# Hybrid decoder block on one core: the second feed-forward matmul as seven block products, with its weight sums on VectorE and GpSimd

## What is computed

```python
h = rms_norm(x, g_ffn_norm[l])
x = x + jnp.square(jax.nn.relu(h @ w_ff1[l])) @ w_ff2[l]
```

## Time and profile before

| | us |
|---|---|
| median of 3 runs | 633.36 (633.29 to 633.74) |
| the profiled execution, its own time | 633.49 |
| its span, first to last instruction | 631.8 |
| PE busy | 617.6 (98%) |
| DVE busy | 325.5 (52%) |
| ACT busy | 264.6 (42%) |
| POOL busy | 11.0 (2%) |

### The profile page before, as it was taken

The page is one execution under the profiler, slowest core; times in us unless marked ns, Lnnn a source line. Parts: engine busy times, 40 slices in busy tenths (PEclk is TensorE's granted clock), DMA queues, the critical chain, the costliest instruction groups (busy, mean ns, idle before and its releaser), DMA issues.

```text
span 631.8 us, 8695 instructions
## 1 busy us (share of the span) xinstructions
PE 617.6 (98%) x3130; PEld 515.5 (82%) x3130; DVE 325.5 (52%) x577; ACT 264.6 (42%) x503; POOL 11.0 (2%) x31
## 2 busy tenths in 40 slices
PE   7999999999999999999999999999999999999997
PEld 5888677788898888988888888888888888888885
DVE  5699981686688686564333333334433333333323
ACT  7656552737466656462222222223333333222220
POOL 1400000000000000000000000000000000000000
PEclk9999999999999999999999999999999999999999
DMA  8512447342121020004223322332222323322003
GB/s 341 181 42 66 134 137 262 102 167 67 34 68 67 0 68 1 1 1 139 95 99 100 100 100 100 100 98 94 87 89 100 100 100 100 100 100 97 36 0 134
DMA packets 17228, 60.08 MB, mean 95 GB/s; under 512 B 2144, under 2 KB 2432, under 8 KB 17200
## 3 DMA queue, kind: packets, MB, share of 16 engines
q1 hardware_dynamic: 16416, 57.88, 27.0%
q0 software_dynamic: 640, 1.82, 0.9%
q10 hardware_dynamic: 144, 0.01, 0.0%
HBM read 57.60 MB, written 2.10 MB: 94 GB/s over the span
## 4 chain that ended last, share of the span: by engine, by line
PE 91%; DVE 4%; ACT 2%; issue 1%; POOL 0%; DVEq 0%; ACTq 0%; POOLq 0%
PE ps L317 26%; PE ps L319 25%; PE ps L318 25%; PE ps L1687 4%; PE ps L1675 2%; PE ps L1636 1%; PE ps L1422 1%; PE ps L1545 1%; PE ps L1637 1%; DVE ht_lo L955 1%; PE ps L1508 1%; PE ps L1617 1%; DVE w_lo_sb L933 1%; ACT ht_hi L564 1%; PE ps L1597 1%
## 5 line engine op out<-in xcount | busy, mean ns | idle before, releaser
L317 PE MATMUL ps<-ht_hi,w_hi_sb 128*128 128x512 f32 (+1 forms) x280 | 107.7, 385 | 0.0
L319 PE MATMUL ps<-ht_hi,w_lo_sb 128*128 128x512 f32 (+1 forms) x280 | 107.3, 383 | 0.0
L318 PE MATMUL ps<-ht_lo,w_hi_sb 128*128 128x512 f32 (+1 forms) x280 | 107.3, 383 | 0.0
L317 PE MATMUL ps<-w_hi_sb,a_hi 128*128 128x512 f32 x256 | 99.6, 389 | 0.0
L318 PE MATMUL ps<-w_lo_sb,a_hi 128*128 128x512 f32 x256 | 99.6, 389 | 0.0
L319 PE MATMUL ps<-w_hi_sb,a_lo 128*128 128x512 f32 x256 | 99.6, 389 | 0.0
L317 PE MATMUL ps<-w_hi_sb,ht_hi 128*128 128x512 f32 x192 | 82.1, 427 | 3.0 <-DVE ht_lo L955 1.6
L1293 DVE TENSOR_TENSOR w_lo_sb<-raw,w_hi_sb 128x1024 fp32r<-128x1024 f32 x64 | 78.3, 1225 | 10.2 <-ACT w_hi_sb L809 5.0
L319 PE MATMUL ps<-w_hi_sb,ht_lo 128*128 128x512 f32 x192 | 75.3, 392 | 0.0
L318 PE MATMUL ps<-w_lo_sb,ht_hi 128*128 128x512 f32 x192 | 75.1, 391 | 0.0
L1358 DVE TENSOR_TENSOR act_sb<-act_sb (+1 forms) x32 | 22.2, 692 | 102.8 <-ACT act_sb L891 102.8
(11 more groups left out here) (189 smaller groups left out, 791.0 us busy)
## 6 DMA issues: line engine op xcount, KB each, us to landing
raw<-in_w_ff SPq DMA_DIRECT2D x64, 512.0 KB, 3.4
raw<-in_w SPq DMA_DIRECT2D x24, 512.0 KB, 4.6
xs<-in_x SPq DMA_DIRECT2D x8, 512.0 KB, 6.7
raw<-in_cmp_w SPq DMA_DIRECT2D x8, 512.0 KB, 4.7
out_y<-xs SPq DMA_DIRECT2D x3, 512.0 KB, 2.7
raw<-in_w_c SPq DMA_DIRECT2D x4, 304.0 KB, 2.8
spw_sb<-in_sp_w POOLq DMA_DIRECT2D x1, 512.0 KB, 3.6
grow_ffn<-in_g_ffn POOLq DMA_DIRECT2D x1, 512.0 KB, 3.8
```

The lines of the kernel that those rows point to most:

```text
L317: pe.matmul(out, l_hi, r_hi, start=start, stop=False)
L318: pe.matmul(out, l_hi, r_lo, start=False, stop=False)
L319: return pe.matmul(out, l_lo, r_hi, start=False, stop=stop)
```

## The change

The second matmul is cut into quadrants: rows of the activations in two halves (256 each), the hidden dimension in two halves (16 units of 128 each), output columns in two halves (512 each). One level of Strassen's scheme (Winograd's form) gives the four output quadrants by seven products of quadrant size and sums of quadrants before and after. Unit J of the hidden dimension now stands for rows J and J + 16 of `w_ff2`.

- **Products.** Group 1, sixteen steps: P1, P5, P6, P4 (4 products x 2 row tiles x 3 passes = 24 matmuls of 128x512 a step). Group 2, sixteen steps: P3, P2, P7 (18 matmuls a step). In all 672 matmuls where there were 768.
- **Activation sums.** Kept for all units in `aq` (six pieces of 256 a unit). DVE makes three sums of 256 for each unit while the first matmul runs (`sums`), and one more after each group-1 step (`fourth_sum`).
- **Weight sums, group 1.** For each step three differences of 128x512, in place in `raw`: DVE makes the first (`t1_form`) for the next step, POOL the second and third (each waits for the one before it). Group 2 has one, on DVE (`t3_form`), and loads `w_ff2` once more (768 KB a step).
- **Partial results.** Between the groups P1, P6, P5 and P4 are taken out of PSUM and combined in `part`; four `base` instructions add them into `xs` during group 2.
- The tiles are laid out anew in SBUF; the work before the second matmul is otherwise the same.

The diff, cut to what the change does in time (line numbers of the changed file are those that the extracts below it use):

```diff
+A11, S1, A22, S2, A12, A21 = range(6)
+S4, S3 = S2, A21
+FIRST = slice(A11, S2 + 1)
+SECOND = slice(S4, S3 + 1)
+PRODUCTS = {"P1": (A11, 0, 0, 0), "P5": (S1, 0, 1, 2), "P6": (S2, 1, 0, 4), "P4": (A22, 1, 1, 6),
+            "P3": (S4, 0, 0, 2), "P2": (A12, 0, 1, 0), "P7": (S3, 1, 0, 4)}
+G1, G1_LAST = ["P1", "P5", "P6", "P4"], ["P1", "P6", "P5", "P4"]
+G2, G2_FIRST = ["P3", "P2", "P7"], ["P2", "P3", "P7"]
...
         @block.gpsimd
...
+            with pool.Fori(0, HF // 2) as i:
+                for j in range(2):
+                    a, b = 2 * j, 2 * j + 1
+                    n = i * 4 + 2 * j
+                    pool.wait_ge(raw_in[b], i * 16 + (IN + 16))
+                    pool.wait_ge(t1_made, i * 2 + (j + 1))
+                    pool.tensor_tensor(raw[:, b, b1], raw[:, b, b1], raw[:, a, b2], ALU.subtract).then_inc(t_made, 1)
+                    pool.wait_ge(t_made, n + 1)
+                    pool.tensor_tensor(raw[:, b, b2], raw[:, b, b1], raw[:, b, b2], ALU.subtract).then_inc(t_made, 1)
...
         @block.scalar
...
+            def first_group(j, J):
+                form_hi(2 * j, J * 2 + (U0 - 3), made_1=J + 1)
+                form_hi(2 * j + 1, J * 2 + (U0 - 2), J * 2 + 2)
+                a_high(j, J, FIRST, J * 2 + (U0 - 2), J * 3 + 3)
...
         @block.vector
...
+            def t1_form(j, loaded):
+                a, b = slice(0, 512), slice(512, 1024)
+                dve.wait_ge(raw_in[2 * j], loaded)
+                dve.tensor_tensor(raw[:, 2 * j, b], raw[:, 2 * j, b], raw[:, 2 * j, a], ALU.subtract).then_inc(t1_made, 1)
...
+            def first_group(j, J, nxt):
+                form_lo(2 * j, J * 2 + (H0 + 1))
+                form_lo(2 * j + 1, J * 2 + (H0 + 2))
+                nxt()
+                a_low(j, J, FIRST, J + 1)
+                fourth_sum(J, J + 1)
...
+            def second_group(j, i):
+                J = i * 2 + (HF + j)
+                form_lo(2 * j, J * 2 + (H0 + 1))
+                form_lo(2 * j + 1, J * 2 + (H0 + 2), 512)
+                t3_form(1 - j, i * 16 + (T3_IN + 16 * j))
+                a_low(j, i * 2 + j, SECOND, J + 1)
...
+            with dve.Fori(1, HF // 2 - 1) as i:
+                first_group(0, i * 2, lambda: t1_form(1, i * 16 + (IN1 + 16)))
+                first_group(1, i * 2 + 1, lambda: t1_form(0, i * 16 + (IN1 + 32)))
+            first_group(0, HF - 2, lambda: t1_form(1, IN1 + 16 * (HF // 2)))
+            first_group(1, HF - 1, lambda: t3_form(0, T3_IN))
+            second_group(0, 0)
+            dve.wait_ge(p1_kept, 1)
+            dve.wait_ge(p_whole, 2)
+            dve.tensor_tensor(part[:, :, 1, :], ps[:, 4:6, :], part[:, :, 0, :], ALU.add).then_inc(kept, 1)
...
+            dve.tensor_tensor(part[:, :, 2, :], ps[:, 2:4, :], part[:, :, 1, :], ALU.add).then_inc(kept, 1)
+            second_group(1, 0)
+            dve.wait_ge(w_used, U0 + 2 * HF)
+            dve.tensor_tensor(part[:, :, 1, :], part[:, :, 1, :], ps[:, 6:8, :], ALU.subtract).then_inc(kept, 1)
...
+            for t in range(4):
+                second_group(t % 2, 1 + t // 2)
+                base(t)
...
         @block.tensor
...
+            def step(j, J, products, first=False, last=False):
+                units = [PRODUCTS[p][1] for p in products]
+                pe.wait_ge(al_done, J + 1)
+                for n, p in enumerate(products):
+                    unit = units[n]
+                    if unit not in units[:n]:
+                        pe.wait_ge(w_lo, J * 2 + (NS + NF + 1 + unit))
...
+                    for i in range(2):
+                        mm = piece(j, p, i, first, last)
+                    if unit not in units[n + 1:]:
+                        mm.then_inc(w_used, 1)
```

More of the change, by code:

```diff
@@ new lines, in _ @@
+                if j % 2:
+                    a_high(j // 2, j // 2, FIRST, NW + NF - (2, 0)[j // 2], 3 * (j // 2) + 3)
+            with act.Fori(1, HF // 2) as i:
+                for j in range(2):
+                    first_group(j, i * 2 + j)
+            second_group(0, 0)
+            act.wait_ge(p_whole, 1)
+            act.activation(part[:, :, 0, :], ps[:, 0:2, :], ACT.Copy).then_inc(p1_kept, 1)
+            second_group(1, 0)
+            with act.Fori(1, HF // 2 - 1) as i:
+                for j in range(2):
+                    second_group(j, i)
@@ L919, in _ @@
+            for j in range(2):
+                second_group(j, HF // 2 - 1, skew=j == 1)
         @block.vector
@@ new lines, in _ @@
+                if j == 1:
+                    sums(NF // FR - 1, 1)
+                if j % 2:
+                    a_low(j // 2, j // 2, FIRST, j // 2 + 1)
+            sums(NF // FR - 1, FR - 1)
+            for J in range(2):
+                fourth_sum(J, J + 1)
+            t1_form(0, IN1 + 32)
+            with dve.Fori(1, HF // 2 - 1) as i:
+                first_group(0, i * 2, lambda: t1_form(1, i * 16 + (IN1 + 16)))
+                first_group(1, i * 2 + 1, lambda: t1_form(0, i * 16 + (IN1 + 32)))
@@ L1399, in _ @@
+            dve.wait_ge(based, 4)
+            for n, (p, i) in enumerate(ENDED):
+                dve.wait_ge(m_done, n + 1)
+                for c in LAST_COLS if n == len(ENDED) - 1 else [slice(0, 512)]:
+                    result(p, i, c)
         @block.tensor
@@ new lines, in _ @@
+            step(0, 0, G1, first=True)
+            step(1, 1, G1)
+            with pe.Fori(1, HF // 2 - 1) as i:
+                for j in range(2):
+                    step(j, i * 2 + j, G1)
+            step(0, HF - 2, G1)
+            step(1, HF - 1, G1_LAST, last=True)
+            step(0, HF, G2_FIRST, first=True)
+            step(1, HF + 1, G2)
+            with pe.Fori(1, HF // 2 - 1) as i:
+                for j in range(2):
+                    step(j, i * 2 + (HF + j), G2)
+            seen = set()
@@ L1812, in _ @@
+            for n, (p, i, e) in enumerate(LAST_TWO):
+                unit, J = PRODUCTS[p][1], 2 * HF - 2 + e
+                if e not in seen:
+                    pe.wait_ge(al_done, J + 1)
+                    seen.add(e)
+                if (e, unit) not in seen:
+                    pe.wait_ge(w_lo, 2 * J + NS + NF + 1 + (unit if e == 0 else 1 - unit))
+                    seen.add((e, unit))
+                mm = piece(e, p, i, False, e == 1)
+                if e:
                     mm.then_inc(m_done, 1)
@@ L1844, in layouts @@
     wo = i["w_out"][0]
+    w2 = i["w_ff2"][0].reshape(NF, P, D)
     return {
```

264 lines of the change are left out of this document (168 added, 96 removed).

## The result

The changed kernel takes 637.25 us (median of 6 runs, 636.27 to 638.02) against 633.37 (633.28 to 634.64) for the kernel before: a ratio of 1.0057, interval 1.0042 to 1.0071. It removes 96 matmuls worth 21.8 us and is 0.6% **slower**. The profiled execution took 637.98 us by its own time.

What follows compares the result with a forecast made beforehand. PE alone was taken to bound the second matmul, and the feeding group 1 after the change. 633.5 - 21.8 (matmuls) + 25.5 (group 1, with step 2's 3.7) + 2.8 (group 2) = 640.0 us; range 624 to 655.

Steps and rivals of the forecast that it cites:

- The mechanism: Second matmul, group 1: POOL and DVE exclude each other, so feeding becomes the bound; PE idles 1.2 to 2.2 us a step.
- Matmuls removed, -21.8: Second matmul: 96 of 768 matmuls removed at 0.2267 us each, all on the path, -21.8 us.
- the ring: Group-1 cycle of waits: POOL's pair, ACT's hi copy, DVE's second lo, `t1_form`, POOL's next pair; 7.1 us against PE's 5.44.
- POOL's duration h: Group 1: time of one POOL difference of 512, bounded by 0.95 and 1.56 us, taken as 1.1.
- Whether POOL and DVE block each other: Group 1: two-SBUF-input DVE instructions and POOL's take turns by whole instructions, read from one encounter in the trace before.
- Rival 1: Group 1: POOL and DVE do not hinder each other, ring 5.44 us, total 617.3 us; chance 0.16.
- POOL first: Group-1 ring: POOL's second difference goes ahead of DVE's first lo; next cycle at 6.6 us, total 633.1.
- DVE first: Group-1 ring: DVE's first lo goes ahead of POOL's second difference; next cycle at 7.65 us, total 647.0.
- Step 2 late, +3.7: Start of group 1: step 2's feeding is ready at 467.6, PE has ended steps 0 and 1 at 463.9; +3.7 us.
- Group 2, +2.8: First group-2 steps: seven extra 1024-element DVE instructions on `part` and `base` make steps 4.6 us; +2.8, between 1 and 6.
- Hidden, priced at nothing: First-matmul sums, POOL's pairs for steps 0 and 1, ReLU in two pieces, second `w_ff2` load: all hidden, 0 us.
- Tail, +-0.3: After the last matmul: a 256-column `result` and its 2.6 us DMA, the same two last as before; +-0.3 us.

Runs made afterwards that it cites:

- the run with 32 columns: The changed kernel with POOL's two differences on 32 columns in place of 512, waits kept: 619.71 us, ratio 0.977 to the kernel before.
- the run with aligned tiles: The changed kernel with 64 bytes left free ahead of the two weight tiles, so they start on multiples of 128: 632.39 us, ratio 0.9967.
- no GpSimd in the same order: The changed kernel with POOL's two differences moved to DVE, right behind the first one, order otherwise kept: 629.06 us, ratio 0.9913.
- earlier first difference: The changed kernel with DVE's difference for the next step put between the two weight lo parts, except at step 15: 635.21 us, ratio 1.0015.

## Where the prediction was right, where it was off, and what was luck

The mechanism was right, with its place and its engine, and 640.0 was 2.8 us too high, with the truth inside the range. That it came out slower, as forecast, was luck: what the mechanism and group 2 cost as measured is under the 21.8 us that the removed matmuls give, and with its weight tiles on multiples of 128 the same kernel is slightly faster than before. The sign and most of the closeness come from a cost that the forecast had priced at nothing.

- **Matmuls removed, -21.8:** as priced. The count of instructions (3034 against 3130) stands; so does the 5.44 us of PE's own work in a step, but for the tiles (5.60 in the odd steps, hidden by the ring).
- **POOL's duration h, taken 1.1 between 0.95 and 1.56:** 1.30 alone (443.76), and 1.13 to 1.16 counted from the moment that DVE lets go, which is what the ring's sum needed. The estimate worked out from the Trainium skill (GPSIMD Engine Reference, Elementwise: side-by-side cycle accounting), 1.12, agrees with the latter.
- **Whether POOL and DVE block each other:** yes, and by whole instructions, as the one encounter had said. The rule in the Trainium skill (SBUF — State Buffer, Who interferes with whom) holds in every meeting seen here. Rival 1 (617.3) falls with it, and the run with 32 columns is near what it would have given.
- **The ring, taken 7.1 a step:** this is **the term that was mis-sized**. The forecast had worked out 6.6 for POOL first and 7.65 for DVE first and took the middle (7.1; its sum has 5.44 + 1.68 = 7.12), since the rows before don't decide the order. It is 6.66: POOL's second is issued 0.08 us after its first ends (506.87 against 506.79), not 0.15 to 0.24 as the earlier trace rows gave, and so 0.13 ahead of DVE's lo. In every meeting read here the one that was issued first got the turn. The middle was worth 13 x 0.46 = 6.0 us too much. A middle of two discrete orders is a time that neither gives; by the forecast's own "POOL first" the sum was 633.1.
- **Step 2 late, +3.7:** 3.6. What the forecast did not have: behind this hole PE runs at its lower level for a while (granted clock 0.87 in the window of steps 2 and 3, whose 48 matmuls take 12.57 us from first to last start instead of 47 x 0.2267 = 10.65). It cost nothing, as the ring sets 13.3 us for two steps anyway.
- **Group 2, +2.8:** 2.25, made of 1.55 for the instructions on `part` and `base` and 0.7 for the tiles. With `base` a step lasts 4.40 us on DVE, not 4.6 (see below), so such a step costs 0.3, not 0.5.
- **Hidden, priced at nothing:** the sums, ReLU in two pieces and POOL's first pairs hide as foreseen. But "The tiles are laid out anew in SBUF; the work before the second matmul is otherwise the same" was a step priced at nothing, without a reason, that costs 3.75 us ahead of the second matmul and 0.7 in group 2, which is what the run with aligned tiles gained. It made good most of the 6.0 that the ring was taken too high: two errors that nearly cancel.
- **Tail, +-0.3:** -0.8.

Put together: 633.5 - 21.8 + 3.6 + 15.8 + 2.25 - 0.8 = 632.6, with the 3.4 by which the second matmul starts later 636.0 (the tiles cost 3.75 there, so the rest of the new layout and order gives back some 0.3), and in the executions with the slower start up to 1.6 more: 637.6 against 637.98 of the profiled one.

One step of DVE near the start of group 2, from `base` to `base`, which gives the 4.40. Timeline of DVE after:
```profile
572.50 1.29 DVE L1571 SCALAR_TENSOR_TENSOR xs<-part,rstd,xs 128x1024 f32<-128x1024 f32 x1
573.70 1.83 DVE L1494 TENSOR_TENSOR w_lo_sb<-raw,w_hi_sb 128x1024 fp32r<-128x1024 f32 x2
575.44 0.69 DVE L1510 TENSOR_TENSOR raw<-raw 128x512 f32<-128x512 f32 x1
576.04 0.96 DVE L1482 TENSOR_TENSOR a_lo<-aq,a_hi 128x768 fp32r<-128x768 f32 x1
576.91 1.29 DVE L1571 SCALAR_TENSOR_TENSOR xs<-part,rstd,xs 128x1024 f32<-128x1024 f32 x1
```
From start to start: 1.20 + 1.74 + 0.60 + 0.87 = 4.41. The forecast took 1.28 for `base` and 0.96 for the 768 elements, which are durations; what a full queue pays is the distance of starts, some 0.09 less for each (so the forecast's "by starts" does not hold for its 0.96).

## What to carry to other kernels

Work that is moved from VectorE to GpSimd "beside it" is not beside it when both read two SBUF operands: add the two engines' times, and take GpSimd's share at its own slower rate (1.14 us against 0.72 here); the better way was to keep it on VectorE and weave it between instructions that others wait for. When a bound depends on which of two orders occurs, forecast the likelier order and put the other into the range, not the mean of both. And before a new kernel is judged by its arithmetic, compare the addresses of its matmul operands with those of the old one: moving the weight tiles by 64 bytes cost the kernel before more (7.4 us) than the change under study did.

## What the runs showed of the hardware

- **Matmul pace depends on how its operands lie to each other modulo 128 bytes.** Of 512 columns in this type: 226.7 ns from start to start when both lie on a multiple of 128 or both 64 beyond it; 228.8 when only the stationary one is 64 beyond; 233.3 to 233.5 when only the moving one is. That is 0.9% and 2.9 to 3.0%, with no wait, no lower clock (1.00 in that whole matmul) and hardly a longer duration in the records to show it: only the distance of starts tells. By what mechanism stays open.
- **In each meeting read the turn went to the instruction issued first,** even by 0.13 us (506.87 on POOL, 507.00 on DVE). Strict alternation of the two engines would give the same order in all of them, so which of the two rules holds is not shown. At a meeting the waiting one ends its own working time after the other's end: 1.13 to 1.16 for POOL's 512, 1.08 for DVE's 1024, 0.28 for DVE's 256.
- **PE's clock after a hole.** After the hole at step 2 (3.6 us from start to start) the granted clock was 0.64 on average over the next 4.8 us, which is some 3.4 us of them at 1.2 GHz and the rest at 2.4, where PE had been for over 440 us; the runs with 3.0 to 4.7 us from start to start there have such a stretch (no GpSimd in the same order 3.0, tiles aligned 3.8, earlier first difference 4.7), the one with 1.1 us (32 columns) has none, nor have the later steps of group 1 with up to 1.3 us between starts where they meet. The window, of the kernel after:
```profile
472.40:477.20 4.80, 4.72 (x14) 3.72 (x15) 4.64 (x4) 2.00 (x2) 2.41 (x2) 0.64 0.29 95
```
